# A two-layer streaming encoder: the norms and the pooling mixer moved in among the last units of the input projection, and the first two units of each layer multiplied on rows that are not yet normalised

## The reference, cut to what is computed

```python
def rmsnorm(x, g):
    y = x * lax.rsqrt(jnp.mean(x * x, axis=-1, keepdims=True) + EPS)
    return y * g
# per layer, h = rmsnorm(x, norm_mix):
qa, ka, va, ub, cq, ckv, kpe, ud, gate_in = split_cols(h @ lw['w_in'])
ud  = ud[..., :512] * jax.nn.sigmoid(ud[..., 512:])     # branch D: GLU, then causal depthwise conv of 31 taps,
o_d = jax.nn.silu(layernorm(conv31(ud) + conv_b, ln_g, ln_b))      #   LayerNorm, swish
o_b = pool_mix(ub, ...)                                 # branch B: trailing means over 2/4/8/16 rows, one matmul a group
o_a = windowed attention of qa, ka, va                  # branch A
o_c = latent attention of rmsnorm(cq), rmsnorm(ckv), rope(kpe)     # branch C
x += (sum over branches of sigmoid(G_b h) * (o_b @ w_o_b)) @ w_out
x += (silu(rmsnorm(x) @ wg) * (rmsnorm(x) @ wu)) @ wd
```

## Time and profile before

| | us |
|---|---|
| median of 3 runs | 2405.38 (2404.38 to 2407.51) |
| the profiled execution, its own time | 2410.11 |
| its span, first to last instruction | 2408.3 |
| TensorE busy in it | 2270.8 |
| VectorE busy | 1302.2 |
| GpSimd busy | 949.3 |
| ScalarE busy | 860.8 |

### The profile page before, as it was taken

How to read it: one execution, slowest core, us unless ns; L and a number is a source line. 1 busy time by engine, 2 the same in 40 slices (tenths; PEclk the granted TensorE clock), 3 DMA queues, 4 the chain that set the end, 5 groups by cost and what they waited for, 6 DMA issues and landing times.

```text
span 2408.3 us, 39646 instructions
## 1 busy us (share of the span) xinstructions
PE 2270.8 (94%) x14968; PEld 2179.9 (91%) x14968; DVE 1302.2 (54%) x2344; ACT 860.8 (36%) x1676; POOL 949.3 (39%) x988
## 2 busy tenths in 40 slices
PE   5997999999999999999989979999999989999996
PEld 5996999788999999999889969988889989999996
DVE  6996243333347835727389752533332487275364
ACT  2014333444314534526311152334442245254352
POOL 3552455232464332323445425542326623333331
PEclk9999999999999999999999989999999999999998
DMA  5241222011232221222224302211112312223221
GB/s 183 84 161 52 68 71 65 29 40 40 81 103 79 71 92 67 97 66 79 96 94 138 114 34 66 70 53 40 40 36 92 109 62 88 79 79 97 67 79 57
DMA packets 70417, 187.79 MB, mean 78 GB/s; under 512 B 19680, under 2 KB 22336, under 8 KB 69248
## 3 DMA queue, kind: packets, MB, share of 16 engines
q1 hardware_dynamic: 53536, 163.27, 20.7%
q10 hardware_dynamic: 16736, 22.52, 2.8%
HBM read 173.46 MB, written 14.14 MB: 78 GB/s over the span
## 4 chain that ended last, share of the span: by engine, by line
PE 87%; DVE 8%; issue 2%; ACT 2%; ACTq 0%; DMA 0%; SPq 0%; DVEq 0%
PE gemm L640 43%; PE gemm L1051 17%; PE gemm L1041 14%; PE side L1051 3%; PE side L924 2%; PE side L904 1%; DVE rstd L1607 1%; DVE act_lo L2034 1%; PE side L710 1%; PE side L855 1%; PE side L911 1%; DVE prod L1636 1%; DVE prod L1790 1%; PE side L782 1%; DVE x L1793 1%
## 5 line engine op out<-in xcount | busy, mean ns | idle before, releaser
L620 POOL TENSOR_TENSOR ring_lo<-w_raw,ring_hi 128x512 fp32r<-128x512 f32 x232 | 307.8, 1329 | 590.7 <-ACT ring_hi L1469 590.7
L603 POOL CAST w_hi<-w_raw 128x384 fp32r<-128x384 f32 x376 | 212.1, 564 | 803.1 <-PE gemm L640 783.7
L640 PE MATMUL gemm<-h_hi,w_hi 128*128 128x320 f32 x1728 | 431.2, 331 | 21.7 <-DVE h_lo L1613 17.0
L605 POOL TENSOR_TENSOR w_lo<-w_raw,w_hi 128x384 fp32r<-128x384 f32 x376 | 432.7, 1151 | 30.1
L640 PE MATMUL gemm<-h_hi,w_lo 128*128 128x320 f32 x1728 | 395.6, 310 | 0.0
L640 PE MATMUL gemm<-h_lo,w_hi 128*128 128x320 f32 x1728 | 395.5, 310 | 0.0
L640 PEld LDWEIGHTS gemm<-h_hi,w_hi 128*128 128x128 f32 x1728 | 294.3, 190 | 53.4 <-issue 39.5
L1051 PE MATMUL gemm<-act_hi,ring_hi 128*128 128x320 f32 x960 | 299.9, 312 | 18.9 <-issue 10.0
L1051 PE MATMUL gemm<-act_hi,ring_lo 128*128 128x320 f32 x960 | 299.1, 312 | 0.0
L1051 PE MATMUL gemm<-act_lo,ring_hi 128*128 128x320 f32 x960 | 299.0, 311 | 0.0
L640 PEld LDWEIGHTS gemm<-h_hi,w_lo 128*128 128x128 f32 x1728 | 290.6, 189 | 0.0
(11 more groups left out here) (276 smaller groups left out, 4168.8 us busy)
## 6 DMA issues: line engine op xcount, KB each, us to landing
w_raw<-in_ws_ff SPq DMA_DIRECT2D x120, 512.0 KB, 3.3
w_raw<-in_ws_gate SPq DMA_DIRECT2D x64, 512.0 KB, 3.3
w_raw<-in_ws_in SPq DMA_DIRECT2D x44, 512.0 KB, 3.3
w_raw<-in_ws_proj SPq DMA_DIRECT2D x64, 256.0 KB, 2.6
w_raw<-in_ws_out SPq DMA_DIRECT2D x16, 512.0 KB, 3.3
w_raw<-in_ws_fd SPq DMA_DIRECT2D x16, 384.0 KB, 3.0
x_park<-x ACTq DMA_DIRECT2D x2, 2560.0 KB, 12.7
x<-x_park ACTq DMA_DIRECT2D x4, 1280.0 KB, 5.8
```

The lines of the kernel that those rows point to most:

```text
L603: eng.tensor_copy(w_hi[s][:, cols], w_raw[s][:, cols]).then_inc(w_high.sem, 1)
L605: eng.tensor_tensor(w_lo[s][:, cols], w_raw[s][:, cols], w_hi[s][:, cols].bitcast(F32), ALU.subtract).then_inc(w_split.sem, 1)
L620: eng.tensor_tensor(lo, src, hi.bitcast(F32), ALU.subtract).then_inc(lo_plain.sem, 1)
L640: mm = eng.matmul(dst[:, hf, 0:HALF], w, r[:, k, cols], start=first and k == 0 and part == 0, stop=last and k == kk - 1 and part == 2)
```

## The change

1. **Units 0 and 1 on raw rows.** ACT makes xu_hi = x * gain (`x_high`) and DVE xu_lo (`x_low`) without rstd. In layer 0 this happens in the loop that squares x; in layer 1 in the loop over the last eight down-projection units of layer 0. PE runs unit 0, then unit 1, on them. The norm's sum stands behind unit 0 in layer 0, and ahead of its tile 4 in layer 1. DVE multiplies the two results by rstd out of PSUM (`first_out`) into `sg` and `value0`; ACT's first sigmoid is then in place on `sg`, ahead of ten DMA issues that stood before it.
2. **Units 2 and 3** are multiplied side by side, unit 3 one tile behind, as h comes.
3. **Weaving.** The `lnm` sums go after tile 2 of unit 19; `lnv`'s, `ckvn`'s and two pool groups in among units 20 and 21; pool group 2 and `cqn` in among merge pair 0, pool group 3 ahead of tile 8 of merge pair 1. Pool results get four buffers of their own (planes of x's buffer, which then holds nothing), so they wait for no reader. On DVE the order becomes: pool 0, centring, kpe's rotation, pool 1, pool 2, LayerNorm, branch D's split, ckv's norm, cq's norm, merge 0, pool 3, merge 1. ACT's order follows.
4. **Seven output DMAs** of keys and values move from ACT's queue to SP's, behind the cache loads. In layer 0 the first two weight loads move up among the loads of x.
5. **Feed-forward norm.** The gained x is no longer written to t2: ACT makes hu_hi from x with a scale, DVE makes hu_lo from x in one instruction. One instruction of DVE a tile goes.

```diff
 # PE
-                layer_norm_sum(l, 0)
-                psum(0, 0)
-                psum(1, 0)
-                for k in range(KT):
-                    h_tile(0)(k)
-                    for s in range(2):
-                        product(l, s, G[s], s, k, KT, h_hi, h_lo)
-                with eng.Fori(1, A_UNITS // 2) as i:
+                for u in range(2):
+                    psum(u, 0)
+                    for k in range(KT):
+                        if u == 0:
+                            eng.wait_ge(xu_ready.sem, xu_ready.at(l, k + 1))
+                            if l and k == KT // 2:
+                                layer_norm_sum(l, 0)
+                        product(l, u, G[u], u, k, KT, xu_hi, xu_lo)
+                    if u == 0 and l == 0:
+                        layer_norm_sum(l, 0)
+
+                for k in range(KT + 1):
+                    if k < KT:
+                        if k == 0:
+                            psum(0, 1)
+                        h_tile(0)(k)
+                        product(l, 2, G[0], 0, k, KT, h_hi, h_lo)
+                    if k:
+                        if k == 1:
+                            psum(1, 1)
+                        product(l, 3, G[1], 1, k - 1, KT, h_hi, h_lo)
+                with eng.Fori(2, A_UNITS // 2 - 2) as i:
...
-                colsum("lnm", [y[:, t, :] for t in range(4)], lambda n: None)
-                for g in range(4):
-                    eng.wait_ge(pooled.sem, pooled.at(l, g + 1))
...
-                    merge_tiles(0, 2 * g, 2 * g + 2)
-                colsum("ckvn", *sq_tiles(0, 1), square=True)
-                colsum("lnv", *sq_tiles(1, 4), square=True)
-                colsum("cqn", *sq_tiles(5, 2), square=True)
-                merge_tiles(0, 8, 12)
-                merge_tiles(1, 0, 12)
+                unit_tiles(18, 0, KT)
+                unit_tiles(19, 0, 3)
                 evacuated(eng, l, ("conv", 3))
                 evacuated(eng, l, "convs")
+                for n in range(4):
+                    colsum("lnm", [y[:, t, :] for t in range(4)], n)
+                unit_tiles(19, 3, KT)
+                lnv = sq_tiles(0, 4)
+                unit_tiles(20, 0, 1)
+                colsum("lnv", lnv, 0, 0)
+                colsum("lnv", lnv, 1, 0)
+                unit_tiles(20, 1, 3)
+                colsum("lnv", lnv, 2, 0)
+                unit_tiles(20, 3, 5)
+                colsum("lnv", lnv, 3, 0)
+                unit_tiles(20, 5, 7)
...
+                pool(0)
+                unit_tiles(20, 7, KT)
+                unit_tiles(21, 0, 3)
+                pool(1)
+                unit_tiles(21, 3, 6)
+                colsum("ckvn", sq_tiles(4, 1), 0, 4)
+                unit_tiles(21, 6, KT)
+                merge_tiles(0, 0, 5)
+                pool(2)
+                merge_tiles(0, 5, 7)
+                colsum("cqn", sq_tiles(5, 2), 0, 5)
+                colsum("cqn", sq_tiles(5, 2), 1, 5)
+                merge_tiles(0, 7, 12)
+                merge_tiles(1, 0, 8)
+                pool(3)
+                merge_tiles(1, 8, 12)
 # ACT
+            def x_high(l, k):
+                eng.activation(xu_hi[k][:, :], x[:, k, :], ACT.Copy, scale=gmix[:, l * KT + k:l * KT + k + 1])\
+                   .then_inc(xu_high.sem, 1)
...
+                queries_out(3)
+                stds(l, lambda hf: ("ckvn", hf), P)
+                square(6, cq[:, 1, :], 0)
+                pool(2)
+                merge_gate(0)
+                eng.wait_ge(ckv_ready.sem, ckv_ready.at(l, 1))
                 stds(l, lambda hf: ("cqn", hf), 2 * P)
                 merge_gate(1)
+                pool(3)
 # DVE
+            def x_low(l, k):
+                eng.wait_ge(xu_high.sem, xu_high.at(l, k + 1))
+                eng.scalar_tensor_tensor(xu_lo[k][:, :], x[:, k, :], gmix[:, l * KT + k:l * KT + k + 1],
+                                         xu_hi[k][:, :].bitcast(F32), ALU.mult, ALU.subtract).then_inc(xu_ready.sem, 1)
...
             for k in range(KT):
+                x_low(0, k)
                 add_square(0, -1, k)
...
+                def first_out(u, dst):
+                    eng.wait_ge(unit_done.sem, unit_done.at(l, u + 1))
+                    for hf, cols in halves:
+                        eng.tensor_tensor(dst[:, cols], rstd[:, cols], G[u][:, hf, 0:HALF], ALU.mult)\
+                           .then_inc(g_free[u].sem, 1)
+                first_out(0, sg)
...
+                    if k == 1:
+                        first_out(1, value0)
...
                 def glu(i):
+                    if i == 0:
+                        read_unit(eng, l, 1)
+                        eng.wait_ge(gate0.sem, gate0.at(l, 1))
+                        eng.wait_ge(conv_hist.sem, conv_hist.at(l, 16))
+                        eng.tensor_tensor(cvp[:, 0, CH:CH + NP], sg[:, 0:NP], value0[:, 0:NP], ALU.mult)
+                        eng.tensor_tensor(cvs[:, 0, :, CH:CH + NQ], heads(sg[:, NP:T]), heads(value0[:, NP:T]), ALU.mult)\
+                           .then_inc(glu0.sem, 1)
+                        return
...
+                scaled(l, 2, lambda hf: ("ckvn", hf))
+                eng.scalar_tensor_tensor(ckvT[:, :], ckvT[:, :], vec[:, V_CKVN:V_CKVN + 1], rstd[:, :],
+                                         ALU.mult, ALU.mult).then_inc(ckv_ready.sem, 1)
                 scaled(l, 3, lambda hf: ("cqn", hf))
                 for t in range(2):
                     eng.scalar_tensor_tensor(cq[:, t, :], cq[:, t, :], vec[:, V_CQN + t:V_CQN + t + 1], rstd[:, :],
                                              ALU.mult, ALU.mult).then_inc(cq_ready.sem, 1)
                 merge(0, 0, first=True)
-                read_unit(eng, l, 13)
-                eng.tensor_tensor(kper[:, :], kper[:, :], cs[0:64, :], ALU.mult).then_inc(kpe_rot.sem, 1)
+                pool(3)
                 merge(1, 1, first=True)
...
                 for m in range(KT):
                     add_to_x(A_UNITS + 2 * M_PAIRS + m, m)
-                    eng.tensor_scalar(t2[m % 2][:, :], x[:, m, :], vec[:, V_GFFN + m:V_GFFN + m + 1], None, ALU.mult)\
-                       .then_inc(t_ready.sem, 1)
                     if m:
-                        h_low(l, 1, m - 1)
+                        hu_low(l, m - 1)
                         add_square(l, 0, m - 1)
...
                         if c == 2:
                             if m:
                                 add_square(l, 1, m - 1)
+                                if l + 1 < L:
+                                    x_low(l + 1, m - 1)
```

More of the change, by code:

```diff
@@ L688, in _, with unit_tiles @@
                         products(l, i * 2 + s, G[s], s, KT, h_hi, h_lo)
+                def unit_tiles(u, first, last):
+                    for k in range(first, last):
+                        if k == 0:
+                            psum(u % 2, u // 2)
+                        product(l, u, G[u % 2], u % 2, k, KT, h_hi, h_lo)
                 def merge_tiles(n, first, last):
@@ L702, in merge_tiles @@
                             product(l, unit + 1, G[1], 1, t - KT, 4, o_hi, o_lo)
-                def colsum(name, tiles, waits, square=None):
-                    for n, tile in enumerate(tiles):
-                        waits(n)
-                        for hf, cols in halves:
-                            if n == 0:
-                                fill(l, (name, hf))
-                            mm = eng.matmul(B[4 + hf][:, 0:HALF], ones[:, :], tile[:, cols],
-                                            start=(n == 0), stop=(n == len(tiles) - 1))
-                            if n == len(tiles) - 1:
-                                mm.then_inc(side.sem, 1)
-                        if square is not None and n < len(tiles) - 1:
-                            mm.then_inc(sq_used.sem, 1)
@@ L717, in sq_tiles, with colsum @@
-                def sq_tiles(first, n):
-                    return [sq[(first + k) % 2] for k in range(n)], \
-                        lambda k: eng.wait_ge(sq_ready.sem, sq_ready.at(l, first + k + 1))
+                def colsum(name, tiles, n, square=None):
+                    if square is not None:
+                        eng.wait_ge(sq_ready.sem, sq_ready.at(l, square + n + 1))
+                    for hf, cols in halves:
+                        if n == 0:
+                            fill(l, (name, hf))
+                        mm = eng.matmul(B[4 + hf][:, 0:HALF], ones[:, :], tiles[n][:, cols],
+                                        start=(n == 0), stop=(n == len(tiles) - 1))
+                        if n == len(tiles) - 1:
+                            mm.then_inc(side.sem, 1)
+                    if square is not None and n < len(tiles) - 1:
+                        mm.then_inc(sq_used.sem, 1)
@@ new lines, in sq_tiles, with pool @@
+                def sq_tiles(first, n):
+                    return [sq[(first + k) % 2] for k in range(n)]
+                def pool(g):
```

(19 more changed lines are left out.)

199 lines of the change are left out of this document (113 added, 86 removed).

## The result

| | us, median of 5 runs | lowest to highest | profiled execution | its span | mean granted clock |
|---|---|---|---|---|---|
| before | 2405.68 | 2404.38 to 2407.51 | 2410.11 | 2408.3 | 0.981 |
| after | 2393.63 | 2391.05 to 2394.54 | 2394.54 | 2392.7 | 0.978 |

The ratio is 0.9948, with a 95% interval of 0.9937 to 0.9959. The change makes the kernel 12 us faster; 26 were forecast, and 2393.6 lies above the range, which ended at 2391. Between the two profiled executions the difference is 15.6 us of span.

What follows compares the result with a forecast made beforehand. VectorE's conv was taken to become the gate of the norms and pool, with a 65 us woven stage behind it. Gains of 8.7 us in layer 0 and 17.6 in layer 1, 26 off 2405.4, gave 2379; range 2368 to 2391.

Steps and rivals of the forecast that it cites:

- bounds 0 and 7.6, taken 3: Layer 0's head: VectorE time lost to GpSimd splitting two units' weights, put at 3 us between 0 and 7.6.
- 1.8 for the clock: Behind the wait for pool 3: 3.5 us of TensorE work at half speed loses 1.8 us.
- the step from the profiled execution to the median: Profiled execution of before taken as 4.7 us above the median, so 26 us came off 2405.4 for 2379.
- The gate: Ahead of the `lnm` sums: VectorE's conv, a block of 117.0 us, ends last, by 1.5 to 3.4 us over TensorE.
- The conv's start in layer 0: Head of layer 0: the conv starts at 52.1 us against 45.97 before, and ends at 169.1 against 169.4.
- The conv's start in layer 1: Head of layer 1: the conv starts at 1228.6 us against 1229.45 and ends at 1345.6, 7.3 earlier.
- The woven stage: Conv's end to kpe sums: 65 us against 75.4 and 77.1 before, with TensorE waiting 7 us for pool 3.
- the bound of 70: Upper bound in us, conv's end to kpe sums, if collisions stretch VectorE's groups and `lnm` starts at half clock.
- (b): Rival: VectorE collides with GpSimd, 4.6 us more in layer 0's head, 4 per woven stage: 2386 to 2392; chance 0.22.
- (c): Rival: holes hold TensorE at 1.2 GHz through the woven stage, 56 us a layer, end near 2470; chance 0.04.
- (a): Rival: the pool 3 stall is absent or halved, up to 9 us more gain a layer: 2361 to 2370; chance 0.15.
- (d): Rival: nothing changes, conv later than thought in both layers and a longer chain behind: 2401 to 2410; chance 0.04.

Runs made afterwards that it cites:

- two halves alone: Changed kernel with both layers' heads as before: 2394.3 us, ratio 0.9953; kernel before with the other edits but its old order of norms and pool: 2402.7 us, 1.0000.
- `glu(1)` early: Changed kernel with `glu(1)` after 12 instructions of the conv in place of 24, in both layers: 2396.2 us, ratio to before 0.9959.
- the conv shortened: Changed kernel with taps 1 to 5 of the conv's prompt on 64 of 512 columns, sums left incomplete: 2376.1 us, ratio to before 0.9889.
- pool 3 moved: Changed kernel with pool 3 and merge 0 ahead of cq's norm on VectorE: 2371.7 us, ratio to before 0.9863.
- the split held: Changed kernel with GpSimd's split of unit 1's weights in layer 0 waiting for VectorE's last add of squares: 2391.6 us, ratio to before 0.9950.
- the last run: Changed kernel with layer 0's old head, `lnm` sums behind unit 19, pool 3 ahead of ckv's and cq's norms, layer 1's `glu(1)` after 12 conv instructions: 2364.1 us, 0.9831.

## Why the prediction missed, step by step

The mechanism came as forecast: the conv gates, and pool 3 stalls. What failed are sizes. The collisions with GpSimd ahead of the conv, "bounds 0 and 7.6, taken 3" in layer 0 and nothing in layer 1, took 5.5 us and 3.2. Half clock, "1.8 for the clock" a layer, took 2.8 and 2.2 behind pool 3 and 1.8 and 1.6 more in the `lnm` sums, for which the sum had nothing. And the step from the profiled execution to the median, carried over whole, was 3.5 us off.

**The gate.** Right. The `lnm` sums start at the end of the conv's last instruction in both layers, VectorE is busy for 117.01 and 116.90 us ahead of them (forecast 117.0), and the three waits of `glu` are gone. TensorE's wins at the head went where the prediction sent them, into waits of 2.8 to 3.2 us ahead of unit 5 and 1.9 to 3.2 ahead of the sums (forecast 4 and 1.5 to 3.4). The two halves alone and `glu(1)` early show it.

**The conv's start in layer 0.** Forecast 52.1 us, measured 54.85. The failing term is "bounds 0 and 7.6, taken 3": eight passes of 0.88 and seven adds of 0.81 are 12.7 us, the block took 18.6 with 0.4 of waiting, so 5.5 us were lost beside GpSimd's splits, and holding one split gave 3.9 of them back (the block took 14.7, from 8.38 to 23.08). The first part of unit 2's split, at 23.2 us, was not in the 7.6 at all.

**The conv's start in layer 1.** 1227.18 is 33.4 us after VectorE takes up the last down-projection unit (1193.74); the forecast was 1228.6 - 1197.23 = 31.4. Here collisions weren't counted, and GpSimd splits units 1 and 2 from 1202.9 to 1212.3 beside the h_lo passes and products: one h_lo took 1.63 us for 0.83, a product 2.17 for 0.89, and two products 2.75 for 1.68. These lose 3.2 us, of which 1.1 came back in small steps elsewhere. No run took the splits away here, so this share is read from the trace and not tested.

**The woven stage.** Forecast 65 us, measured 67.7 and 66.9. The order, the stall of 7.0 us and its place were as forecast. Two sizes of the clock were off: the 1.8 us behind pool 3 were 2.8 and 2.2, and the `lnm` sums at half clock (6.24 and 6.07 us) stood only in the bound of 70. From their start to the first pool sum it is 20.94 and 20.77 us, and 19.15 with the conv shortened, where they ran at full clock: 1.8 and 1.6 us.

| | forecast gain | measured | off |
|---|---|---|---|
| layer 0: conv's start | -6.1 | -8.9 | 2.8 |
| layer 0: stage (with the conv's 117.0) | 14.8 | 12.2 | 2.6 |
| layer 0, to the kpe sums | 8.7 | 3.3 | 5.4 |
| layer 1, on its own | 17.6 | 13.8 | 3.8 |
| behind the kpe sums of layer 1 | 0 | -1.5 | 1.5 |
| sum, by the profiled executions | 26.3 | 15.6 | 10.7 |

The 1.5 us behind are no part of the change. From the kpe sums of layer 1 to the second chunk of the feed-forward it is 627.4 us in the changed kernel's profiled execution and 626.4 in the one of before; with the same code in that stretch it is 624.0 to 624.4 in seven experiments (and 624.2 with edit 5 undone), and 624.8, 626.1 and 626.4 in three. The traces show what differs: the granted clock behind the same holes. TensorE waits 2.66 us, 370.4 us behind the kpe sums, in all of them; in the 9 us from 366 us on the mean granted clock is 0.70 in layer 1 of the changed kernel and 0.71 before, but 0.81 in layer 0 of the same execution and with pool 3 moved, and in the next 5 us it is 0.85, 0.84 and twice 1.00. TensorE comes to its next hole 1.2 us sooner at the higher clock, and the rest is lost in the same way behind the holes from 541 us on. What decides the clock there no run settled.

**From the profile to the median.** Another 3.5 us. The profiled execution of before lay 4.4 us above the median and outside its five runs (up to 2407.51), that of after 0.9. The prediction carried the first figure over whole, as though both executions were equally high. Executions of the kernel before ranged from 2401 to 2410 over all these runs, so this alone could move the answer by 4 us, and the range had no term for it.

**The rivals.** No case came out alone. Of the 10.7 us that the trace is short, 4.9 are collisions ahead of the conv, that is (b), given 0.22. The rest of both layers is 4.3, and half clock beyond the forecast explains all of it: 1.0 and 0.4 behind pool 3, 1.8 and 1.6 in the `lnm` sums, 4.8 in all. No rival had it at this size; (c) had it for the whole stage. With half clock in both `lnm` sums added to (b)'s own bounds the range would have reached 2395. (a), no stall at pool 3, did not come, though one move makes it true; (c) and (d) did not come. (c)'s price doesn't come out of its own terms either: 56 us in each layer on top of 2379 is 2491, where it said near 2470.

How a collision works can be read from one pass. It starts at 19.62, with a subtraction of GpSimd under way from 19.10 to 21.10. If it could only begin its work at 21.10, it would end 0.87 later, at 21.97; it ended at 21.77. The Trainium skill (SBUF — State Buffer, SBUF: two separate sides) has the shared ports locked for a whole instruction while the other engine blocks. The trace agrees within 0.2 us. The conv, which has one input in SBUF and its accumulator in PSUM, shows no such stretches: its prompt taps took 0.75 to 0.77 us each beside a GpSimd that was busy for 64.75 of 117.1 us.

**Edit 5 and the DMAs on SP.** Forecast at nothing. Edit 5 undone gave the same time, and of the DMAs the profile shows nothing: TensorE's only wait for GpSimd's split weights is the 6.3 us at the head of layer 0, and its waits for the weights that VectorE splits in the feed-forward are 8.3 us, against 8.9 before.

## What to carry to other kernels

When work is pulled forward onto an engine with idle time, ask which engine now ends last in that stretch. Here what TensorE won ahead of the conv came back as waits. The largest gain, 20 us, was one move in VectorE's order behind the conv: what another engine waits for goes ahead of what is only needed a stage later.

Price collisions by what the second engine does in exactly those microseconds, its next unit's work included, and price a stall with the half clock behind it: 7.0 us of waiting cost 9.8 in layer 0 here, and 9.3 in layer 1.

A profiled execution and a median are two numbers. Give the step from one to the other a term in the range.

## What the runs showed of the hardware

- After a hole of 1.9 us ahead of the `lnm` sums they ran at half clock in some places (6.24 us, layer 0 of the changed kernel) and at full clock in others (4.54, both layers with the split held, and after a hole of 3.14 in the last run). The same program point with the same hole gave both, and these runs don't settle what decides it. The same holds behind the hole of 2.66 us, 370 us behind the kpe sums: over the 9 us around it the mean granted clock is 0.81 in layer 0 and 0.70 in layer 1 of one execution of the changed kernel, on the same code.
- Behind the 7.0 us stall the lower level (1.2 GHz) was there in both layers of every kernel that had it: 2.50 us for four matmuls that take 1.24 without the stall.
- A collision costs both sides: beside VectorE's passes GpSimd's subtractions of 640 columns took 2.00 us, and 1.54 at 28.07 us, where VectorE waited for ScalarE.
